# Attention heads that begin in the phase before and end among the chunks of the phase after

## The reference, cut to what matters

```
p = softmax(where(picked and causal, q.k * 128**-0.5, -inf))
out = ((p @ v) * silu(gate)) @ w_out
```

## Time and profile before

| | |
|---|---|
| median of 3 runs | 2426.16 us (2425.68 to 2426.28) |
| the profiled execution | 2423.46 us |
| its span in the trace | 2421.7 us |
| busy: PE, DVE, ACT | 97%, 64%, 46% |
| granted PE clock, mean | 0.99 of full speed |

### The profile page before, as it was taken

How to read it: one execution, slowest core, us unless ns; L and a number is a source line. 1 busy time by engine, 2 the same in 40 slices (tenths; PEclk the granted TensorE clock), 3 DMA queues, 4 the chain that set the end, 5 groups by cost and what they waited for, 6 DMA issues and landing times.

```text
span 2421.7 us, 31105 instructions
## 1 busy us (share of the span) xinstructions
PE 2346.1 (97%) x10938; PEld 1896.5 (78%) x10938; DVE 1545.3 (64%) x1863; ACT 1116.3 (46%) x1339; POOL 15.2 (1%) x21
## 2 busy tenths in 40 slices
PE   5999999999999989999998999998999999999997
PEld 1877777788778768888787888887888888888886
DVE  1988897666696566875765444665565555555555
ACT  1454445444444445545444444444544444444444
POOL 0000000000000000000000000000000000000000
PEclk9999999999999999999999999999999999999999
DMA  9999996555697436756454766555556655655652
GB/s 394 376 376 383 376 400 222 166 176 181 214 374 245 139 144 195 226 159 190 129 176 138 235 193 193 181 195 182 165 187 193 193 185 190 191 188 189 192 185 104
DMA packets 245062, 527.95 MB, mean 218 GB/s; under 512 B 20956, under 2 KB 21220, under 8 KB 241000
## 3 DMA queue, kind: packets, MB, share of 16 engines
q1 hardware_dynamic: 241376, 510.40, 62.7%
q0 software_dynamic: 1936, 13.67, 1.5%
q10 hardware_dynamic: 1656, 2.65, 0.3%
HBM read 520.35 MB, written 6.30 MB: 217 GB/s over the span
## 4 chain that ended last, share of the span: by engine, by line
PE 90%; DVE 5%; DMA 2%; issue 2%; ACT 1%; DVEq 0%; ACTq 0%; SPq 0%
PE ps L1852 28%; PE ps L1854 28%; PE ps L1853 28%; PE ps L1921 2%; DMA T<-in_mod_w 2%; DVE wide L1257 1%; PE ps L1951 1%; DVE w_lo L1018 0%; PE ps L2124 0%; DVE tmp L1474 0%; ACT tmp L802 0%; PE ps L2022 0%; PE ps L2097 0%; DVE stage L1496 0%; PE ps L2145 0%
## 5 line engine op out<-in xcount | busy, mean ns | idle before, releaser
L1018 DVE TENSOR_TENSOR w_lo<-raw,w_hi 128x1024 fp32r<-128x1024 f32 x784 | 945.0, 1217 | 487.9 <-ACT w_hi L513 470.7
L513 ACT CAST w_hi<-raw 128x1024 fp32r<-128x1024 f32 x784 | 814.5, 1047 | 857.3 <-PE ps L1854 784.4
L1852 PE MATMUL ps<-w_hi,xa_hi 128*128 128x512 f32 x2176 | 855.7, 393 | 10.2 <-DVE w_lo L1018 3.7
L1854 PE MATMUL ps<-w_hi,xa_lo 128*128 128x512 f32 x2176 | 848.1, 390 | 0.0
L1853 PE MATMUL ps<-w_lo,xa_hi 128*128 128x512 f32 x2176 | 847.6, 390 | 0.0
L1852 PEld LDWEIGHTS ps<-w_hi,xa_hi 128*128 128x128 f32 x2176 | 409.1, 188 | 106.8 <-issue 12.9
L1854 PEld LDWEIGHTS ps<-w_hi,xa_lo 128*128 128x128 f32 x2176 | 408.9, 188 | 86.0
L1853 PEld LDWEIGHTS ps<-w_lo,xa_hi 128*128 128x128 f32 x2176 | 409.2, 188 | 82.3
L1852 PE MATMUL ps<-w_hi,xb_hi 128*128 128x512 f32 x928 | 366.2, 395 | 2.9 <-DVEq L1498 1.4
L1854 PE MATMUL ps<-w_hi,xb_lo 128*128 128x512 f32 x928 | 362.2, 390 | 0.0
L1853 PE MATMUL ps<-w_lo,xb_hi 128*128 128x512 f32 x928 | 362.1, 390 | 0.0
(11 more groups left out here) (259 smaller groups left out, 978.2 us busy)
## 6 DMA issues: line engine op xcount, KB each, us to landing
raw<-in_w_in SPq DMA_DIRECT2D x176, 512.0 KB, 4.2
T<-in_mod_w SPq DMA_DIRECT2D x160, 512.0 KB, 7.8
raw<-in_attn_w_in SPq DMA_DIRECT2D x144, 512.0 KB, 4.5
raw<-in_w_up SPq DMA_DIRECT2D x128, 512.0 KB, 4.5
raw<-in_w_down SPq DMA_DIRECT2D x128, 512.0 KB, 4.2
raw<-in_pool_w_in SPq DMA_DIRECT2D x64, 512.0 KB, 8.2
T<-in_mod_w SPq DMA_DIRECT2D x16, 1024.0 KB, 8.9
raw<-in_pool_w_out SPq DMA_DIRECT2D x32, 512.0 KB, 8.2
```

Source lines behind the costliest of these rows:

```text
L513: nc.scalar.copy(w_hi[:, o % SPL, :, 0:cols], raw[:, o % RAW, :, 0:cols]).then_inc(hi_ready, 1)
L1018: tt(w_lo[:, o % SPL, :, part], raw[:, o % RAW, :, part], w_hi[:, o % SPL, :, part].bitcast(F32), ALU.subtract).then_inc(lo_ready, 1)
L1852: mm(dst, x_hi, h, start=first and k == 0, stop=False)
L1854: ins = mm(dst, x_lo, h, start=False, stop=last and k == KPC - 1)
```

## The change

The order of two phases is exchanged: `gate` (now to T2, with the rider and the Silu evacuation) stands before `v` (now to T3). The four blocks of `v` are written out instead of looped. `top_k` runs once after each block of `gate`, and four times in the first two blocks of `v`; `picks` runs in the third.

In all three attentions logits 0 and 1 stand behind c4 and c5 of the last block of the phase before, their masks (and for the mLSTM their divisors) at DVE's steps 7 and 8 there, and their exps at ACT's steps 9 and 10. The chunks c0 and c1 of the next phase are put behind PV of the last two heads, and c2 behind them (`fill`); its first block then starts at c3 (`at=3`, `ahead=AHEAD + 2`). PV uses the two banks that the next phase's first sum does not.

Per head, the mask's instruction scales by -scale and takes the minimum, so that `nmx` is gone; the exp takes scale -1. The waits of DVE for itself inside a mask and inside a division are gone; the reciprocal stands before the mask and is waited for after it. The jobs of the attentions use `split_job` and `low_job`: `leave` is gone. The first job of MoBA moves from the attention into the first block of `g_m` (behind c3, its second behind c5), and heads 4 to 7 go to `stage2`, in `wide`. The mLSTM's jobs move from behind c1 and c3 of `a_qk` to behind c5 and c7, with DVE's parts at steps 7, 8 and 10 instead of 4 and 6, and ACT's at 8 and 10 instead of 4 and 6. The exp tables are loaded before `v` and before `a_v`.

```diff
-RIDERS = {"v": 5}
+RIDERS = {"gate": 5}
...
+            def exps(h, i):
+
+                act.wait_ge(masked, h + 1)
+                for t, (a, z) in enumerate(((0, P), (P, CAUS))):
+                    nc.scalar.activation(
+                        probs[:, i % 2, a:z], probs[:, i % 2, a:z], ACT.Exp, bias=mx[:, i % 2, t:t + 1],
+                        scale=-1.0, accum_out=den[:, i % 4, t:t + 1])
+                act.drain()
+                act.sem_inc(exp_ready, 1)
+
+            def exp_hooks(h0):
+                return {9: lambda: exps(h0, 0), 10: lambda: exps(h0 + 1, 1)}
+
+            def attention(h0, heads, name, jobs, B):
+
+                for i in range(1, heads + 2):
+                    if 2 <= i < heads:
+                        exps(h0 + i, i)
+                    if i <= heads:
                         copy_probs(h0 + i - 1, i - 1)
-                    if i >= 6 and i % 4 == 2 and i < heads:
+                    if i >= 6 and i % 4 == 2 and i < heads and jobs:
                         n = (i - 6) // 4
-                        split(JOBS[name] + n, SPLITS[name] + n, XA, g0 + n, x_tmp)
-
-            attention(0, 0, DSA_HEADS, "attn", 0)
+                        split_job(JOBS[name] + n, SPLITS[name] + n, XA, n, 2)
+                    if i >= heads:
+                        hi(B, AHEAD + i - heads)
+
...
+            attention(0, DSA_HEADS, "attn", True, PHASES["attn_out"][0])
...
+            phase("a_qk", to_stage("a_qk", scale=r_mix), first={8: mlstm_split(0), 10: mlstm_split(1)}, ahead=AHEAD + 2)
...
+            def picks():
+                step(ts(score, score, 0.5 * (TAKEN + FAR), UNPICKED, ALU.is_gt, ALU.mult))
+                step(tt(pick[:], score, tri, ALU.add))
+
+            def mask(h, i, of):
+
+                dve.wait_ge(lg_ready, h + 1)
+                if i >= 2:
+                    dve.wait_ge(pt_ready, h - 1)
+                for t, (a, z) in enumerate(((0, P), (P, CAUS))):
+                    ins = nc.vector.tensor_tensor_reduce(
+                        out=probs[:, i % 2, a:z], in0=ps[:, 4 + i % 2, a:z], in1=of[:, a:z], scale=-(HD ** -0.5),
+                        scalar=-FAR, op0=ALU.add, op1=ALU.min, accum_out=mx[:, i % 2, t:t + 1])
+                ins.then_inc(masked, 1)
+
+            def mask_hooks(h0, of):
+                return {7: lambda: mask(h0, 0, of), 8: lambda: mask(h0 + 1, 1, of)}
+
+            def attention(h0, e0, heads, name, of, gate, bank, jobs, B):
+
+                for i in range(2, heads + 2):
+                    j = i - 2
+                    b = j % 2
+                    dve.wait_ge(exp_ready, e0 + j + 1)
+                    nc.vector.reciprocal(rden[:, b, :], den[:, j % 4, :]).then_inc(rden_ready, 1)
                     if i < heads:
-                        h, b = h0 + i, i % 2
-                        dve.wait_ge(lg_ready, h + 1)
-                        if i >= 2:
-                            dve.wait_ge(pt_ready, h - 1)
-                        for t, (a, z) in enumerate(((0, P), (P, CAUS))):
-                            step(nc.vector.tensor_tensor_reduce(
-                                out=probs[:, b, a:z], in0=ps[:, 4 + b, a:z], in1=mask[:, a:z], scale=1.0,
-                                scalar=FAR, op0=ALU.add, op1=ALU.max, accum_out=mx[:, b, t:t + 1]))
-                        ts(nmx[:, b, :], mx[:, b, :], -(HD ** -0.5), None, ALU.mult).then_inc(masked, 1)
-                    if i >= 6 and i % 4 == 2 and i < heads:
-                        n = (i - 6) // 4
-                        leave(JOBS[name] + n, x_tmp, bank=2)
-                    if i >= 6 and i % 4 == 3 and i < heads:
-                        low_part(SPLITS[name] + (i - 7) // 4, XA, g0 + (i - 7) // 4, x_tmp)
-                    if 2 <= i < heads + 2:
-                        j = i - 2
-                        b = j % 2
-                        dve.wait_ge(exp_ready, e0 + j + 1)
-                        if name == "attn" and j == 0:
-                            dve.wait_ge(acc_free, PHASES["gate"][1] + 4)
-                        step(nc.vector.reciprocal(rden[:, b, :], den[:, j % 4, :]))
-                        dve.wait_ge(pv_ready, h0 + j + 1)
-                        for t in range(NT):
-                            dst, src = stage[:, t, j % 4 * HD:j % 4 * HD + HD], ps[:, b, t * HD:t * HD + HD]
-                            if gate is None:
-                                step(ts(dst, src, rden[:, b, t:t + 1], None, ALU.mult))
-                            else:
-                                step(stt(dst, src, rden[:, b, t:t + 1], gate[:, t, j * HD:j * HD + HD],
-                                         ALU.mult, ALU.mult))
-                        dve.sem_inc(o_done, 1)
-                        if j % 4 == 3:
-                            dve.sem_inc(staged, 1)
-
...
+                        mask(h0 + i, i, of)
+                    dve.wait_ge(rden_ready, e0 + j + 1)
+                    if name == "attn" and j == 0:
+                        dve.wait_ge(acc_free, PHASES["v"][1] + 4)
+                    dve.wait_ge(pv_ready, h0 + j + 1)
+                    for t in range(NT):
+                        dst, src = (stage if jobs or j < 4 else stage2)[:, t, j % 4 * HD:j % 4 * HD + HD], ps[:, bank + b, t * HD:t * HD + HD]
+                        if gate is None:
+                            ins = ts(dst, src, rden[:, b, t:t + 1], None, ALU.mult)
+                        else:
+                            ins = stt(dst, src, rden[:, b, t:t + 1], gate[:, t, j * HD:j * HD + HD],
+                                      ALU.mult, ALU.mult)
+                    ins.then_inc(o_done, 1)
+                    if j % 4 == 3:
+                        dve.wait_ge(o_done, h0 + j + 1)
+                        dve.sem_inc(staged, 1)
+                    if jobs and i >= 6 and i % 4 == 3 and i < heads:
+                        low_job(SPLITS[name] + (i - 7) // 4, XA, (i - 7) // 4, 2)
+                    if i >= heads:
+                        lo(B, AHEAD + i - heads)
+
+            B0, A0, n = PHASES["v"]
+            for b in range(n):
+                blk(B0 + b, ({5: top_k}, {5: top_k}, {5: picks}, mask_hooks(0, pick[:]))[b])
+                if b < 2:
+                    top_k()
...
-                  first={2: lambda: mlstm_stage(0), 4: mlstm_mid, 6: mlstm_last})
...
+                  first={2: lambda: mlstm_stage(0), 7: mlstm_mid, 8: lambda: mlstm_low(0), 10: mlstm_last}, ahead=AHEAD + 2)
...
+            def logits(h0, i, q, k, rows_of=1):
+                h = h0 + i
+                if i >= 2:
+                    pe.wait_ge(masked, h - 1)
+                for t, (a, z) in enumerate(((0, P), (P, CAUS))):
+                    for r in range(rows_of):
+                        ins = mm(ps[:, 4 + i % 2, a:z], q(i, r)[:, t * P:(t + 1) * P], k(i, r)[:, 0:z - a],
+                                 start=r == 0, stop=r == rows_of - 1)
+                ins.then_inc(lg_ready, 1)
+
+            def ahead(name, X, ready=None):
+
+                B0, A0, _ = PHASES[name]
+
+                def fill(j):
+                    if j == 0:
+                        pe.wait_ge(acc_free, A0 - 1)
+                        if ready:
+                            pe.wait_ge(tp_evac, JOBS["attn"] + 3)
+                    if ready and j % 2 == 0:
+                        pe.wait_ge(x_ready, ready + j // 2 + 1)
+                    chunk(B0, j, X, KPC * j, A0, j == 0, False)
+                return fill
+
...
+                    if i >= heads:
+                        fill(i - heads)
+                fill(2)
...
-            phase("a_qk", XB, aqk_job, first={1: mlstm_job(0), 3: mlstm_job(1)})
...
+            phase("a_qk", XB, aqk_job, first={5: mlstm_job(0), 7: mlstm_job(1)}, at=3)
...
+            phase("g_m", XB, first={3: moba_job(0, stage, 4), 5: moba_job(1, stage2, 6)}, at=3)
```

More of the change, by code:

```diff
@@ L414, in _ @@
             load_phase("idx_kw", cols=80)
-            for name in ("qk", "v", "gate", "attn_out", "m_qk"):
+            for name in ("qk", "gate", "v", "attn_out", "m_qk"):
                 if name == "m_qk":
@@ L561, in blk, with phase @@
                         hooks[o]()
-            def phase(name, each, job=None, at=6, first=None):
+            def phase(name, each, job=None, at=6, first=None, ahead=AHEAD):
                 B0, A0, n = PHASES[name]
-                blk(B0, first)
+                blk(B0, first, at=ahead)
                 each(0, B0, A0)
@@ L778, in _ @@
                 to_qk(b, b + B0, b + A0)
-            phase("v", lambda b, B, A: evac(T2[:, :, bass.ds(b * NBLK, NBLK)], A, B * CPB + CPB))
+            phase("gate", lambda b, B, A: evac(T2[:, :, bass.ds(b * NBLK, NBLK)], A, B * CPB + CPB, ACT.Silu))
+            load_table(4, ACT.Exp)
             act.wait_ge(sum_rows, 2)
@@ L1068, in blk, with phase @@
                         hooks[o]()
-            def phase(name, each=None, out=None, low=None, per=0, first=None):
```

(27 more changed lines are left out.)

213 lines of the change are left out of this document (109 added, 104 removed).

## The result

| | before | after |
|---|---|---|
| median of five runs | 2425.68 us (2420.96 to 2426.28) | 2410.55 us (2407.06 to 2411.98) |
| profiled execution / its span | 2423.46 / 2421.7 us | 2410.67 / 2408.9 us |
| ratio of times | | 0.9939, 95% interval 0.9928 to 0.9949 |

Forecast: 2409.4 us, range 2404 to 2416. The page of the changed kernel shows PE at 91% of the chain that ended last (90% in the earlier trace rows). The second fence is from the list of PE's waits: us in total, times, longest. The third is from the same list of the kernel before.

A forecast was written before the change was run, and what follows sets the result against it. PE was taken to bound the kernel (90% of the chain), so savings count only where it waits. Terms -12.3 - 6.1 - 2.6 + 3.7 + 0.5 = -16.8 us took 2423.46 to 2406.7; plus 2.7 for the median, 2409.4, range 2404 to 2416.

The forecast's parts named there:

- DSA, -12.3: DSA attention: entry 2.5, mask(2) to mask(15) 31.2, exit 3.7, so 37.4 us instead of 49.75.
- MoBA, -6.1: MoBA attention: 16.9 us instead of 23.82, less 0.87 for the job moved to `g_m`.
- The pace: DSA and MoBA heads: circle for two heads 4.19 us instead of 4.73, so 2.09 a head instead of 2.36.
- mLSTM, -2.6: mLSTM attention: 11.8 us instead of 14.45, with logits 0 and 1 in the block before.
- The stop in `a_qk`, +3.7: First block of `a_qk`: PE stands still once before c11, waiting for its late `lo`, 3.7 us.
- Silu with the rider, +0.5: `gate` phase: the Silu table load now falls where DVE is nearly full, +0.5 us, ends 0 and 1.3.
- 1 (self-waits cost nothing): DSA and MoBA heads: removing DVE's self-waits gains nothing, 2.30 us a head, +3.8, 2413; chance 0.12.
- 2 (no stop): First block of `a_qk`: PE does not stop there, 2405.7 us; chance 0.07.
- 3 (the stop repeats): All four blocks of `a_qk`: the 3.7 us stop comes in each, 11 us more, 2420.5; chance 0.06.
- 4 (one circle instead of two): DSA and MoBA heads: heads stop interlocking, a head takes the whole 4.19 us, +37.6, 2447; chance 0.05.

The follow-up runs named there:

- buffer: Changed kernel with the three jobs inside the DSA heads leaving PSUM through an SBUF buffer again: -0.06 us in DSA.
- cure: Changed kernel with the mLSTM product's two jobs two chunks earlier in the first block of `a_qk`: 2403.58 us, ratio to the kernel before 0.9915.
- order: Changed kernel with `v` (with the rider) before the Silu gate again: +1.73 us in DSA.
- selfwait: Changed kernel with VectorE's waits for itself back in mask and division: +2.48 us in DSA, +1.41 in MoBA.
- old_entry: Changed kernel with the old entry of DSA and MoBA (phase order, last search and pick, logits, masks, exps, exp table): +4.34 us in DSA, +2.31 in MoBA.
- half: Changed kernel with the mLSTM product's two jobs one chunk earlier in the first block of `a_qk`: 2405.30 us, one run.
- entry: Changed kernel with logits, masks and exps 0 and 1 behind the last chunk of the phase before: +1.23 us in DSA, +1.06 in MoBA.
- recip: Changed kernel with the reciprocal behind the mask again in DSA and MoBA: +0.52 us in DSA, +0.28 in MoBA.
- exit: Changed kernel with the next phase's three chunks behind the last division in all three attentions: +2.18 us in DSA, +2.22 in MoBA.
- nmx: Changed kernel with the negated maximum, as its own instruction with one self-wait, back in DSA and MoBA: +1.34 us in DSA, +0.59 in MoBA.

## Why the prediction was right, point by point

- *DSA, -12.3: measured -13.3.* Entry and exit came as worked out (1.18 us to mask(2), 3.18 us to c0, both within 0.1); the pace gave the rest, 30.02 us for the thirteen steps instead of 31.2. What jobs and semaphores add to the bare pace was right (30.02 less 13 x 1.99, half of the measured circle, is 4.1, forecast 4.0), but that a job loses `leave` is worth nothing (buffer).
- *MoBA, -6.1: measured -6.3.* Entry 1.15. A circle took 3.98 us, 1.99 a head, where the price was 2.09; five paces with the semaphore of the fourth head took 10.30, forecast 10.65.
- *The pace.* The forecast took off 0.21 a head for self-waits and 0.10 for `nmx` (0.21 a circle), and put on 0.04 for the reciprocal ahead of the mask. The runs gave, over the four heads of MoBA, 0.18, 0.10 (8.66 less 8.27, over four), and for the reciprocal 0.02 gained instead of 0.04 lost. Mask(2) to mask(6) took 9.55 us before and 8.27 after, 0.32 a head less, so 0.30 of 0.32 is accounted for.
- *mLSTM, -2.6.* c0 starts 7.66 us after transposes(0) (1146.40 and 1154.06), worked out as 7.9. If cure's 6.70 is all that the stop cost, the rest of the change gave 6.70 - 3.81 = 2.9 here.
- *The stop in `a_qk`, +3.7: the wait was 3.92, but the term measured 6.7.* This is the term that was mis-sized. The mechanism was right: one wait, before c11, in the first block alone. Counted from the end of c5 (1171.93), the rotation started at 12.7 (worked out: 12.8), the `lo` was ready at 19.4 (19.2), and PE wanted it at 15.5 (15.4). What was left out is that PE comes back from such a wait at the lower clock, though the earlier trace rows showed 0.75 in DSA's entry behind a wait of 3.7 us. Cure took back 6.70.
- *Silu with the rider, +0.5: 0.* From the last stage transposes ahead of `qk` to the last chunk ahead of the heads it was 167.23 us before and 168.59 after (662.02 to 830.61), in which eight matmuls of logits now stand, 1.3 us. That leaves nothing for Silu. In order, with the rider in `v`, the same distance is 168.60.
- *Rivals.* 1 (self-waits cost nothing) is refuted by selfwait; 2 (no stop) and 3 (the stop repeats) by the one wait of 3.9; 4 (one circle instead of two) by the pace.

The sum of the terms was -16.8 and the stretches gave -15.9: the stretches of DSA, MoBA and mLSTM gave 1.6 us more than forecast and Silu 0.5, `a_qk` took 3.0 more. The sum was this near by luck, because these misses offset each other; either side alone, 2.1 or 3.0 us, would still have left the time in the range. The median was near by a second piece of luck: between the profiled runs the change gave 12.8, 4.0 less than forecast, most of the difference in code that it doesn't touch, while the forecast had added 2.7 us from the profiled run to the median, and in the changed kernel the median lies 0.1 below the profiled run.

What undoing each part costs adds up in DSA to 4.34 + 2.18 + 2.48 + 1.34 + 0.52 = 10.9 of 13.3; the remaining 2.5 no run took apart. Of these, 0.8 stand in the entry: from the last chunk to mask(2) it is 6.56 us in old_entry and 7.38 in the kernel before, at a granted clock of 0.85 and 0.75. In MoBA the undoings add up to 2.31 + 2.22 + 1.41 + 0.59 + 0.28 = 6.8, 0.5 more than the 6.3 of the change. The job that moved into `g_m` was not moved back in any run, so its share is not known; both kernels pay for its transposes within the stretch that the table measures.

## What to carry to other kernels

Work that is moved out of a latency-bound stretch lands somewhere: count the receiving engine's queue up to its next deadline, in program order. Here this gave the place and length of the new wait in advance, and moving the jobs two chunks earlier took it away (2403.58 us). Where PE would stand still for as long as here (3.5 us and more), add what it loses at the lower clock behind the wait, 1.3 to 2.8 us here. Half's wait of 2.34 us cost nothing more, but a wait of 2.1 us at another place cost 1.4 us more in six of twelve kernels. In a circle over several engines that serves two heads, an instruction or self-wait of 0.1 us counts once a round if nothing else is awaited there; 1.2 us less work in a gap counts nothing.

## What the runs showed of the hardware

**The clock behind the wait in `a_qk`.** The granted clock behind PE's one wait in the first block of `a_qk`, over ten kernels with nearly the same code around it: after 2.34 us none of the chunk's twelve matmuls ran slow; after 3.54 and 3.56 us seven were at the lower level throughout; after 3.86 and 3.91, six and seven; after 3.88 to 3.92, in five others, eleven or twelve. Chunk and job together cost 1.3 to 2.8 us more than in half. Where the clock came back thus differed between runs with the same wait, by up to 1.3 us (old_entry and the changed kernel, 3.91 and 3.92). This fence shows buffer, with the wait and the chunk behind it:

```profile
1187.79:1191.35 3.56, 0.01 (x1) 0.00 (x0) 3.11 (x6) 1.04 (x1) 0.00 (x0) 0.99 0.00 0
1191.35:1195.74 4.39, 4.39 (x13) 3.45 (x14) 2.22 (x2) 0.00 (x0) 0.00 (x0) 0.62 0.72 221
```

The chunk took 4.39 us here and 5.29 in the changed kernel. The wait itself was 0.35 us shorter in selfwait and buffer: there the low parts start 0.34 us behind the rotation, and 0.71 in the changed kernel. Why isn't known.

**A shorter wait, the same code, either clock.** All twelve kernels have a wait of 2.1 us at 451 us of the span, before any code that the change touches, and PE is busy without a pause for over 20 us ahead of it. In six (after, cure, selfwait, buffer, entry, recip) the lower clock stands behind it; in the other six (before, half, order, exit, old_entry, nmx) the clock stays up. First the wait, then six matmuls and eight transposes, in the changed kernel and in order:

```profile
451.38:453.48 2.10, 0.00 (x1) 0.00 (x0) 1.63 (x7) 0.32 (x1) 0.00 (x0) 0.98 0.31 120
453.48:456.41 2.93, 2.93 (x15) 2.93 (x15) 0.42 (x2) 0.32 (x1) 0.00 (x0) 0.50 0.63 175
```
```profile
451.06:453.16 2.10, 0.01 (x1) 0.00 (x1) 1.63 (x7) 0.32 (x1) 0.00 (x0) 1.00 0.27 103
453.16:454.73 1.57, 1.57 (x15) 1.57 (x15) 0.42 (x2) 0.33 (x1) 0.00 (x0) 1.00 0.38 51
```

The same work takes 2.93 us or 1.57. So the length of the wait alone doesn't tell whether the clock falls, and these 1.4 us are more than half of the 2.35 by which before and after differ ahead of the stretches. The waits of 2.95 us and more in the attention stretches and in `a_qk`, eleven in all twelve kernels, all had the lower clock behind them.
